# A decoder step's projection loop: when key and value items ride with the projection steps, and how tightly the decay chain is spaced

## The reference, cut to what matters

```python
qa, ka, va, qb, kc, vc, ks, vs, kw, vw, g = jnp.split(x @ w_in, offsets, axis=-1)
...
past_a = cache_a[page_table].reshape(B, past, 2, N_HEADS_A, HEAD_DIM)
o_a = stick_breaking(qa, jnp.concatenate([past_a[:, :, 0], ka], axis=1),
                     jnp.concatenate([past_a[:, :, 1], va], axis=1), pos, k_pos)
...
def stick_breaking(q, k, v, q_pos, k_pos):
    z = jnp.einsum('bqhd,bkhd->bhqk', q, k).astype(jnp.float32) / math.sqrt(HEAD_DIM)
    mask = k_pos[None, :] < q_pos[:, None]
    log_beta = jax.nn.log_sigmoid(z)
    log_rest = jnp.where(mask, jax.nn.log_sigmoid(-z), 0.0)
    nxt = jnp.concatenate([log_rest[..., 1:], jnp.zeros_like(log_rest[..., :1])], axis=-1)
    after = lax.cumsum(nxt, axis=3, reverse=True)
    w = jnp.where(mask, jnp.exp(log_beta + after), 0.0)
    return jnp.einsum('bhqk,bkhd->bqhd', w.astype(v.dtype), v)
```

## Time and profile before

| | us |
|---|---|
| median of 3 runs | 2491.43 |
| lowest, highest | 2490.02, 2493.76 |
| the profiled execution, its own time | 2487.3 |
| its span, first to last instruction | 2485.4 |
| TensorE busy | 1768.1 (71%) |
| VectorE busy | 1271.0 (51%) |
| granted TensorE clock, mean | 0.794 |

### The profile page before, as it was taken

The page is one execution under the profiler, slowest core; times in us unless marked ns, Lnnn a source line. Parts: engine busy times, 40 slices in busy tenths (PEclk is TensorE's granted clock), DMA queues, the critical chain, the costliest instruction groups (busy, mean ns, idle before and its releaser), DMA issues.

```text
span 2485.4 us, 29982 instructions
## 1 busy us (share of the span) xinstructions
PE 1768.1 (71%) x9899; PEld 971.3 (39%) x9899; DVE 1271.0 (51%) x2384; ACT 355.0 (14%) x805; POOL 823.2 (33%) x595
## 2 busy tenths in 40 slices
PE   8999999979997877778765656869543333355335
PEld 6777766544596655556412213218200000000000
DVE  0500121353588676687947252345899444455651
ACT  0001110431231011111201020022200011021111
POOL 0000000000023443333324232333445776767662
PEclk9999999989998998889887777979655555555556
DMA  9999989987499999999999999999999999999998
GB/s 388 362 356 365 370 325 377 382 329 292 160 417 371 393 405 409 407 407 406 373 388 406 385 381 403 419 421 420 420 421 393 422 421 421 422 422 421 422 422 345
DMA packets 213307, 961.21 MB, mean 387 GB/s; under 512 B 23841, under 2 KB 89378, under 8 KB 122754
## 3 DMA queue, kind: packets, MB, share of 16 engines
q0 software_dynamic: 84432, 626.26, 61.2%
q1 hardware_dynamic: 92914, 300.39, 31.2%
q10 hardware_dynamic: 35808, 32.65, 3.9%
HBM read 952.73 MB, written 14.88 MB: 389 GB/s over the span
## 4 chain that ended last, share of the span: by engine, by line
DMA 41%; PE 38%; DVE 11%; issue 4%; ACTq 2%; POOL 2%; ACT 1%; SPq 1%; POOLq 0%; DVEq 0%
DMA sb<-in_peer_v,sb 25%; PE bank L1109 14%; DMA sb<-in_nsa_t 8%; PE bank L1525 4%; DVE sb L2474 4%; DMA sb<-in_peer_u,sb 4%; PE bank L1800 4%; PE bank L1411 3%; PE bank L1458 3%; PE bank L1180 2%; PE bank L1208 2%; DMA sb<-in_nsa_v 2%; POOL sb L2584 2%; ACTq L440 1%; PE bank L1591 1%
## 5 line engine op out<-in xcount | busy, mean ns | idle before, releaser
L1800 PE MATMUL bank<-sb 128*32 128x512 f32 x2304 | 472.3, 871 | 507.9 <-DMA sb<-in_peer_v,sb 477.1
L2584 POOL DMA_INDIRECT sb<-in_peer_v,sb x288 | 487.9, 1694 | 577.1 <-PE bank L1800 489.2
L2474 DVE CUSTOM_DVE_ANT_1 sb<-sb 128x2048 f32<-128x2048 f32 x192 | 439.7, 2294 | 326.2 <-DMA sb<-in_peer_u,sb 322.2
L2584 POOL DMA_INDIRECT sb<-in_peer_u,sb x288 | 326.9, 1135 | 475.5 <-DVE sb L2474 255.8
L1800 PEld LDWEIGHTS bank<-sb 128*32 128x32 f32 x2304 | 60.5, 127 | 824.5 <-DMA sb<-in_peer_v,sb 752.2
L1109 PE MATMUL bank<-sb 128*128 128x288 f32 x1408 | 351.6, 410 | 7.5 <-DMA sb<-in_tokens_t 7.5
L1525 PE MATMUL bank<-sb 128*128 128x256 f32 x1024 | 279.7, 433 | 86.4 <-DMA sb<-in_nsa_t 77.5
L1109 PEld LDWEIGHTS bank<-sb 128*128 128x128 f32 x1408 | 266.1, 191 | 91.6 <-issue 13.0
L1525 PEld LDWEIGHTS bank<-sb 128*128 128x128 f32 x1024 | 249.1, 310 | 128.4 <-DMA sb<-in_nsa_t 91.4
L2474 DVE CUSTOM_DVE_ANT_0 sb<-sb 128x2048 f32<-128x2048 f32 x96 | 219.9, 2293 | 153.1 <-DMA sb<-in_peer_u,sb 151.5
L1068 ACT ACTIVATE sb<-sb 128x32 f32<-128x32 f32 x288 | 86.4, 316 | 717.1 <-PE bank L1800 418.3
(11 more groups left out here) (377 smaller groups left out, 1503.9 us busy)
## 6 DMA issues: line engine op xcount, KB each, us to landing
sb<-in_a_k SPq DMA_DIRECT2D x128, 512.0 KB, 7.3
sb<-in_a_v SPq DMA_DIRECT2D x128, 512.0 KB, 7.0
sb<-in_w_in SPq DMA_DIRECT2D x43, 1024.0 KB, 9.2
sb<-in_w_out SPq DMA_DIRECT2D x32, 1024.0 KB, 6.7
sb<-in_w_query SPq DMA_DIRECT2D x32, 1024.0 KB, 9.6
sb<-in_nsa_t SPq DMA_DIRECT2D x200, 128.0 KB
sb<-in_nsa_t ACTq DMA_DIRECT2D x184, 128.0 KB
sb<-in_nsa_v SPq DMA_DIRECT2D x64, 128.0 KB
```

What stands on the lines that cost most here:

```text
L1800: mm = pe.matmul(bank[g % 2][32 * c:32 * c + 32, :], diag[j % 4], rows[:, 512 * c:512 * c + 512], start=(s in FIRST), stop=(s in LAST), sk ...
L2474: dve.tensor_tensor_reduce(out=u, in0=u, in1=replica(g), scale=1.0, scalar=0.0, op0=ALU.mult, op1=ALU.add, accum_out=act16[:, r % 2, j:j + ...
L2584: pool.indirect_dma_start(rows[j % 4], None, dram[table], bass.IndirectOffsetOnAxis(ap=idx, axis=0)).then_inc(full[j % 4], 16)
```

## The change

Five tables of the loop are rewritten. Key items ran in two of every three steps (9, 10, 12, 13, ... 31); now they run in four of five (15 to 18, 20 to 23, 25 to 28), so that the sixteenth is at step 28 and not 31. The units' copies and transposes move forward with them. The links of the side chain for the new tokens and of each half's decay chain are placed at most a few steps earlier and mostly one step behind one another. The first half's value items run at steps 30, 31, 33, 34, 36, 37, 39 and 40 and not 34 to 43; steps 41, 42 and 43 then carry no item. No instruction is added or removed (one table load of ScalarE that the order makes necessary is beside one that it makes unnecessary), and what comes after the loop is unchanged.

```diff
-AK_AT = {9 + 3 * i // 2: i for i in range(16)}
-AV_AT = {34: 0, 35: 1, 37: 2, 38: 3, 39: 4, 41: 5, 42: 6, 43: 7}
-UNIT_OUT = {14: 0, 15: 1, 17: 2, 20: 3, 23: 4, 26: 5, 29: 6, 32: 7}
-UNIT_TURN = {30: 0, 31: 1, 32: 2, 33: 3, 38: 4, 39: 5, 40: 6, 41: 7}
+AK_AT = {9: 0, 10: 1, 12: 2, 13: 3, 15: 4, 16: 5, 17: 6, 18: 7, 20: 8, 21: 9, 22: 10, 23: 11, 25: 12, 26: 13, 27: 14, 28: 15}
+AV_AT = {30: 0, 31: 1, 33: 2, 34: 3, 36: 4, 37: 5, 39: 6, 40: 7}
+UNIT_OUT = {14: 0, 15: 1, 17: 2, 19: 3, 22: 4, 24: 5, 27: 6, 29: 7}
+UNIT_TURN = {26: 0, 27: 1, 28: 2, 29: 3, 36: 4, 37: 5, 38: 6, 39: 7}
...
-                if i == 23:
+                if i == 22:
                     act.wait_ge(new_pe, 1)
...
-                elif i == 25:
+                elif i == 23:
                     act.wait_ge(new_dve, 1)
...
-                if i in (22, 34):
+                if i in (21, 31):
                     act.wait_ge(sa_neg, 1 + i // 30)
...
-                elif i in (29, 37):
+                elif i in (25, 34):
                     decay(i // 30)
...
-                elif i == 27:
+                elif i == 24:
                     pe.wait_ge(new_dve, 2)
...
-                if i in (21, 33):
+                if i in (20, 30):
                     decay_start(i // 30)
-                elif i in (24, 35):
+                elif i in (22, 32):
                     decay_soft(i // 30)
-                if i in (28, 36):
+                if i in (25, 33):
                     decay_arg(i // 30)
```

More of the change, by code:

```diff
@@ L756, in front @@
                     act.activation(e_new[0:NSMP], e_new[0:NSMP], ACT.Ln, bias=1.0).then_inc(new_act, 1)
-                elif i == 29:
+                elif i == 27:
                     act.wait_ge(new_dve, 3)
                     act.activation(z_new[0:NSMP], z_new[0:NSMP], ACT.Exp).then_inc(new_act, 1)
-                if i in (22, 34):
+                if i in (21, 31):
                     act.wait_ge(sa_neg, 1 + i // 30)
@@ L1939, in front @@
                     prompt_gelu()
-                elif i == 24:
+                elif i == 23:
                     dve.wait_ge(new_act, 1)
                     ch.tell(dve.scalar_tensor_tensor(out=en, in0=zn, scalar=-1.0, in1=zn, op0=ALU.mult, op1=ALU.min), new_dve, 1)
-                elif i == 26:
+                elif i == 24:
                     dve.wait_ge(new_act, 2)
@@ L1950, in front @@
                         ch.tell(ins, new_dve, 2) if half else ch.do(ins)
-                elif i == 28:
+                elif i == 25:
                     dve.wait_ge(new_pe, 2)
@@ L1954, in front @@
                     ch.tell(dve.tensor_tensor(zn, zn, bank[7][0:NSMP, 0:256].rearrange("p (h n) -> p h n", h=NH), ALU.subtract), new_dve, 3)
-                elif i == 30:
+                elif i == 28:
                     dve.wait_ge(new_act, 3)
```

## The result

| | before | changed |
|---|---|---|
| median, us | 2487.19 (14 runs) | 2492.51 (14 runs) |
| lowest, highest, us | 2482.46, 2495.11 | 2484.48, 2499.32 |
| the profiled execution, its span, us | 2485.4 | 2492.0 |
| projection loop ends (first L1276), us | 458.39 | 462.62 |
| output projection starts (first L1411), us | 588.5 | 592.6 |

The ratio of the changed kernel's time to the kernel before is 1.0019, with a 95% interval of 1.0010 to 1.0028: about 4.7 us slower (2.5 to 7.0). The forecast was 2.1 us slower, at 2493.5 us. With eleven more runs of the kernel before, its median is 4 us under the one on which the forecast stood. So it is in part luck that the forecast time is within 1 us of the measured one: the difference between the kernels was forecast too small (2.1 us, under the interval's 2.5) and the time of the kernel before too high. The ratio is what counts.

What follows compares the result with a forecast made beforehand. TensorE was taken to bound the projection loop, and transfers the expert stage. Terms 1.8 + 0 + 0.3 = +2.1 us on 2487.3 gave 2489.4; with the three runs' 4.1 us distance the forecast was 2493.5 us, range 2487 to 2499.

Steps and rivals of the forecast that it cites:

- The bound: Projection loop to 458 us: TensorE is busy throughout, so order gains nothing; everything behind starts later by the added 2.1 us.
- The rows of four: Steps 15 to 18, 20 to 23, 25 to 28: loads fall behind, each fourth key item 0.6 us late, +1.8 us.
- The loads' rival: Loads bound the loop's dense part at 392 GB/s: 5.7 us of waits, +6 us in all, 2497.4 us; chance 0.19.
- The ceiling of 365 GB/s: In the loop, 365 GB/s as a limit makes 21 loads take 60.3 us against 54.2: +18 us, 2510; chance 0.03.
- The links: Side and decay chains in the loop one step apart: costed at nothing, with 6 us in hand at step 24.
- Value items 8 and 9 earlier: Behind the loop: their sooner loads gain 0 us, since item 8's release sets the next waits; at most 2 us.
- The seam: At the loop's end, block 43's evacuation stands ahead of the L816 copies TensorE waits for: +0.3 us.
- The faster rival: Stage behind the loop shortens: waits shrink 2 us, clock stays up for 3.4 us; -5.1 us, 2486.3; chance 0.09.

Runs made afterwards that it cites:

- fewer bytes: The changed kernel with each half load of a key item fetching 896 of its 1024 columns; ratio to the kernel before 1.0012 (0.9998 to 1.0026).
- rows of six: The changed kernel with key items 4 to 15 at steps 15 to 20 and 22 to 27; one execution, not timed, waits 4.0 us in total.
- the keys alone: The kernel before with only key items and their units' copies placed as in the change; ratio to the kernel before 1.0017 (1.0005 to 1.0029).
- the links alone: The kernel before with the side chain at the changed steps and the first half's decay chain closed up behind it; ratio 1.0005 (0.9992 to 1.0017).
- the experiment with item 8: The changed kernel with both halves of value item 8 ahead of stick_scores(2); ratio to the kernel before 1.0020 (1.0005 to 1.0034).
- two more items in the loop: Changed kernel, keys three in a row, value items 8 and 9 inside the loop, first half's copies at step 42, output writes later; ratio 1.0021 (1.0009 to 1.0034).
- the copies inside the loop: The changed kernel with ScalarE's two copies of the first half's output (L816) at step 42; ratio to the kernel before 1.0012 (0.9995 to 1.0028).
- rows of three: The changed kernel with key items at 15 to 17, 19 to 21, 23 to 25, 27 to 29, value items from 31 to 41; ratio 0.9999 (0.9984 to 1.0013).

## Why the prediction was right, and where its size was off

- **The bound.** Right. The loop is TensorE's: with enough loads it takes what its matmuls take (458.4 us with fewer bytes). What was waited in the changed loop arrives behind it: L1411 and L1525 both start 4.1 us later, and the timed runs say 4.7 (2.5 to 7.0). Two readings of the rows were off, without weight in the sum: behind slice 12 TensorE falls to seven and eight tenths first, and to three only from slice 31; and 413 GB/s is not the busiest window of the loop, since between 25 and 50 us it is 449.
- **The rows of four.** The mechanism was right and this is the term that was mis-sized: +1.8 us told, 4.0 measured (2.9, 2.7 and 2.6 in three other executions of the same key order). From the third item to the fourth the deficit of 1.15 us holds in the first and third row: 12.69 and 12.73 us of loads against 11.55. In the second it is 13.39, which is why its fourth item waits longest; the reason is not shown. The larger error is a pair earlier. I priced all five loads between the second and third item at 2.54 us, 12.7 us. In the changed trace they take 15.2, 14.7 and 14.4 us: in the first row, the second item's last half load is issued 0.52 us after the row's 161.30 and lands 4.5 us later, at 166.3, and the third item's loads are complete when TensorE starts on it at 181.59.

```profile
161.30 0.85 SPq L635 DMA_DIRECT2D sb<-in_a_k  x2
...
DMA to landing us min/median/max: 3.8/4.1/4.5
```

  I had seen a restart of the queue there ("that window ... holds no restart of the queue") and chose the price of a window without one. A lead of 2.5 to 3.2 us, larger than the 1.7 I had taken, made up for most of it. So third items were just in time or 0.8 late, and fourth items 0.7 to 1.4 late rather than 0.6. What the five loads were slow by is not the rate. These windows of the changed kernel stand ahead of the second item's last landing, between it and the third's, and between the third's and the fourth's:

```profile
156.00:158.00 2.00, 2.00 (x19) 1.23 (x21) 0.00 (x0) 0.41 (x2) 0.00 (x0) 1.00 0.00 0
162.00:163.00 1.00, 1.00 (x6) 0.79 (x5) 0.00 (x0) 0.00 (x0) 0.00 (x0) 1.00 0.60 147
166.29:181.45 15.16, 14.46 (x109) 9.99 (x107) 1.89 (x9) 1.07 (x3) 0.00 (x0) 1.00 1.01 410
181.45:194.14 12.69, 11.62 (x96) 8.38 (x96) 0.20 (x2) 0.79 (x3) 0.00 (x0) 1.00 1.03 414
```

  The DMA engines stood idle at 156 us and were thinly loaded until 163. From 166.29 on they are full: 15.16 us at 410 GB/s are 6.2 MB, where five loads are 5.24 MB, and 12.69 us at 414 are 5.25 MB. So about 1 MB of loads issued later moved before the last bytes of the third item landed (0.6 MB in the other two rows); in the next 12.69 us the bytes moved are those of five loads. While the queue fills, bytes and rate alone don't give the landing. Why later bytes go ahead, and that the thin queue is the condition for it, was read from the landings and windows and not tried apart.
- **The loads' rival** (392 GB/s throughout, 5.7 us) is out as a rate: the DMA engines moved 401 to 414 GB/s between the landings of second, third and fourth items in all three rows, and in the rows of six a row that is behind is fed at 12.7 us a pair. But one of the signs named for it came, a wait ahead of a third item (0.83 us, and 0.43 with the keys alone), and two of the waits ahead of fourth items are over the 1 us told; so that sign did not tell the two apart. The ceiling of 365 GB/s is out too: slices 4 and 5 of the changed loop ran at 390 and 389. With it goes, for this case, the limit of about 358 GB/s for a core that DMA: Bandwidth & Descriptors (the Trainium skill, Specifications) gives; these slices disagree with it as well. (The slices of the loop before show 325 to 388, not "356 to 370".)
- **The links.** Right, nothing: the kernel with the links alone has no wait in the loop.
- **Value items 8 and 9 earlier.** Right, and closely: the waits for 10 and 11 are 3.85 us together against 3.95, the DMA share falls to 0.25 in the 17 us behind the loop, and the experiment with item 8 shows the release to be what counts. The bound of 2 us was too generous in another way too: with two more items in the loop, 6.6 us less of waits for loads were matched by 6.5 us more of waits for VectorE and ScalarE.
- **The seam.** Right: 0.70 against 0.40 us, and gone with the copies inside the loop.
- **The faster rival** did not come: the clock between 500 and 550 us is granted at 0.86 and 0.87, as before. Its idea that the clock counts in this stage does hold: see the last section.

## What to carry to other kernels

Where a loop keeps one engine full, an order of its extra work can't make it faster, only add waits: ask of a denser order how many loads in a row fall behind, and count a lead from the row's actual landings. Here the queue was thin just before the dense part, and the five loads up to a row's third item took 14.4 to 15.2 us where the steady price gives 12.7; rows of three were free, with little to spare, and rows of four were not. And loads that come sooner are worth nothing when the next ones wait for a release further down a chain of other engines. Where a stage has gaps, look at the granted clock before a longer stage is put down to waiting.

## What the runs showed that was not expected

- The steady price is remarkably exact: 2.54 us for 1 MiB (12.69 to 12.73 us for five, in six places of the kernel with rows of six and in two of three of the changed one; the third is the 13.39 us above).
- Two executions of the same key order wait 4.0 and 2.6 us in the loop, while the loop's matmuls take the same time to some hundredths.
- From the prompt's transposes to the output projection it is 127.2 to 130.5 us in kernels in which the instructions between them are the same. It goes with TensorE's busy time there, and that with the clock: 127.2 us at 102.5 busy and a granted clock of 0.93, 128.2 at 103.9 and 0.92, 130.5 at 106.2 and 0.91; with item 8 at once it is 131.4 at 107.2 and 0.90. A stretch at half the clock in one place or another, behind a wait, is worth more here than the seam.
